# Matmul operands placed 32 and 96 bytes past the 2048-byte remainder of the weight tiles in SBUF

## What is computed

```python
x = x + mixed(mamba(h @ w_in), attention(h @ w_in)) @ w_mix_out
x = x + (silu(h @ w_ffn_gate) * (h @ w_ffn_up)) @ w_ffn_down
h = h + norm(diff_attention(norm(h)))
h = h + norm(conv_ffn(norm(h)))
h = h + norm(forgetting_attention(norm(h), k, v, c))
h = h + norm(conv_ffn(norm(h)))
```

## Time and profile before

| | us |
|---|---|
| median of 3 runs (lowest, highest) | 2476.02 (2474.82, 2476.4) |
| the profiled execution's own time | 2476.41 |
| its span in the trace | 2474.6 |
| TensorE matmul busy | 2439.0 (99%) |
| GpSimd busy | 1618.5 (65%) |
| VectorE busy | 1330.5 (54%) |
| ScalarE busy | 746.7 (30%) |

### The profile page before, as it was taken

How to read it: one execution, slowest core, us unless ns; L and a number is a source line. 1 busy time by engine, 2 the same in 40 slices (tenths; PEclk the granted TensorE clock), 3 DMA queues, 4 the chain that set the end, 5 groups by cost and what they waited for, 6 DMA issues and landing times.

```text
span 2474.6 us, 38549 instructions
## 1 busy us (share of the span) xinstructions
PE 2439.0 (99%) x13513; PEld 2002.5 (81%) x13520; DVE 1330.5 (54%) x1980; ACT 746.7 (30%) x1369; POOL 1618.5 (65%) x1548
## 2 busy tenths in 40 slices
PE   9999999999999999999999899999999999999999
PEld 7888888888778888888877688888877777888887
DVE  8777775535326333211555569785173344788822
ACT  3564552011232111101344433331042233333301
POOL 8756665755557777776544368887763434888874
PEclk9999999999999999999999999999999999999999
DMA  5433434333324333333322123333222222333331
GB/s 163 126 90 107 115 100 142 104 82 86 81 73 128 96 95 97 97 97 92 110 64 65 47 82 97 97 97 98 82 86 86 77 65 65 94 97 97 95 97 64
DMA packets 238100, 231.18 MB, mean 93 GB/s; under 512 B 16064, under 2 KB 230592, under 8 KB 237976
## 3 DMA queue, kind: packets, MB, share of 16 engines
q1 hardware_dynamic: 214528, 206.82, 28.7%
q10 hardware_dynamic: 23448, 22.61, 3.3%
HBM read 225.06 MB, written 4.84 MB: 93 GB/s over the span
## 4 chain that ended last, share of the span: by engine, by line
PE 71%; ACT 1%; DVE 1%; issue 0%; DMA 0%; SPq 0%; DVEq 0%; ACTq 0%
PE PS L682 42%; PE PS L673 5%; PE PS L674 5%; PE PS L677 5%; PE PS L666 4%; PE PS L757 3%; PE AUX L1008 2%; PE AUX L1052 1%; PE AUX L1064 1%; PE AUX L1069 1%; PE AUX L785 0%; PE AUX L791 0%; PE AUX L1029 0%; PE AUX L1011 0%; ACT opA_hi L1149 0%
## 5 line engine op out<-in xcount | busy, mean ns | idle before, releaser
L632 POOL TENSOR_TENSOR wlo<-raw,whi 128x512 fp32r<-128x512 f32 x772 | 1063.7, 1378 | 64.4
L630 POOL TENSOR_SCALAR whi<-raw 128x512 fp32r<-128x512 f32 x772 | 557.0, 721 | 766.9 <-issue 418.0
L682 PE MATMUL PS<-opA_hi,whi 128*128 128x512 f32 x1312 | 524.4, 400 | 0.9 <-DVE cu L1595 0.8
L682 PE MATMUL PS<-opA_hi,wlo 128*128 128x512 f32 x1312 | 511.7, 390 | 0.0
L682 PE MATMUL PS<-opA_lo,whi 128*128 128x512 f32 x1312 | 511.0, 390 | 0.0
L682 PEld LDWEIGHTS PS<-opA_hi,whi 128*128 128x128 f32 x1312 | 246.4, 188 | 59.9 <-issue 7.5
L682 PEld LDWEIGHTS PS<-opA_hi,wlo 128*128 128x128 f32 x1312 | 246.2, 188 | 53.0
L682 PEld LDWEIGHTS PS<-opA_lo,whi 128*128 128x128 f32 x1312 | 246.6, 188 | 49.6 <-issue 1.2
L2045 DVE SCALAR_TENSOR_TENSOR facc<-fu,vec,facc 128x512 f32<-128x512 f32 x176 | 216.8, 1289 | 15.8 <-ACT facc L1401 15.8
L673 PE MATMUL PS<-opA_hi,whi 128*128 128x512 f32 x560 | 221.2, 395 | 1.6 <-DVE XT L1900 0.8
L674 PE MATMUL PS<-opA_hi,wlo 128*128 128x512 f32 x560 | 218.6, 390 | 0.0
(11 more groups left out here) (329 smaller groups left out, 3760.4 us busy)
## 6 DMA issues: line engine op xcount, KB each, us to landing
raw<-in_w_in_dram SPq DMA_DIRECT2D x184, 256.0 KB, 2.8
raw<-in_ffn_w_in_dram SPq DMA_DIRECT2D x176, 256.0 KB, 2.8
raw<-in_ffn_w_out_dram SPq DMA_DIRECT2D x88, 256.0 KB, 2.6
raw<-in_a_w_qkv_dram SPq DMA_DIRECT2D x48, 256.0 KB, 2.7
raw<-in_w_ffn_gate_dram SPq DMA_DIRECT2D x44, 256.0 KB, 2.8
raw<-in_w_ffn_up_dram SPq DMA_DIRECT2D x44, 256.0 KB, 2.8
raw<-in_w_ffn_down_dram SPq DMA_DIRECT2D x44, 256.0 KB, 2.7
acs_row<-acs_dram ACTq DMA_DIRECT2D x16, 512.0 KB, 5.8
```

Of the source, the lines that this page charges most:

```text
L630: nc.gpsimd.tensor_scalar(whi[slot][:], raw[raw_slot][:], 1.0, 1.0, ALU.mult, ALU.mult).then_inc(w_high, 1)
L632: nc.gpsimd.tensor_tensor(wlo[slot][:], raw[raw_slot][:], whi[slot][:].bitcast(F32), ALU.subtract).then_inc(slab_split, 1)
L682: last = nc.tensor.matmul(psum_fm(key, panel, m), a, b[:, k, :], start=k + n == 0, stop=k == total - 1 and n == 2)
```

## The change

`opA_at`, the mark behind the weight tiles, stays where it is. `opA_hi` now begins 32 bytes past it, and everything placed in order behind it in the first region moves by 32 bytes with it. `A0` is rounded up to the remainder of `opA_at` plus 96 bytes. `A0` was 128 bytes behind the end of `ident_bf` and is now 192 bytes behind that end, which has itself moved by 32, so that the whole region moves by 96 bytes. `raw`, `whi`, `wlo` and `XT` stay.

| tile | bytes past the weights' remainder by 2048, before | after |
|---|---|---|
| `raw`, `whi`, `wlo` | 0 | 0 |
| `opA_hi`, `opA_lo` | 0 | 32 |
| `yT`, `o1`, `mix`, `hid`, `opB`, `q2`, `k2`, `sc`, `pT` | 0 | 96 |
| `ident` | 320 | 352 |
| `XT` | 1856 | 1856 |

No instruction, wait, transfer or size is added, removed or reordered.

```diff
         KB = 1024
         ROW = 4 * S
+        OPERAND_STEP, REGION_STEP = 32, 96
         BASE = -(-nc.sbuf_base // 64) * 64
...
         opA_at = r.at
+        r.at += OPERAND_STEP
         opA_hi = r.put("opA_hi", [P, DC, S], F32R)
...
         ident_bf = r.put("ident_bf", [P, P], BF16)
-        A0 = r.at + (opA_at - r.at) % ROW
+        A0 = r.at + (opA_at + REGION_STEP - r.at) % ROW
```

## The result

The changed kernel takes 2524.32 us (median of 4 runs, 2522.76 to 2526.18) against 2476.21 for the kernel before (median of 4). The ratio is 1.0185, with a 95% interval of 1.0173 to 1.0197: 48 us slower. The forecast was 19 us faster with a range that ended at 2507, so both the direction and the range were wrong.

What follows compares the result with a forecast made beforehand. TensorE was taken as the bound, through the distance between matmul starts. The profiled 2476.4 us less 19.1 for weight products, all else zero, gave 2457.3, named as 2457; range over all cases 2385 to 2507, likeliest case 2385 to 2471.

Steps and rivals of the forecast that it cites:

- What bounds the kernel: TensorE busy 2439.0 of 2474.6 us at full clock, longest wait sum 5.6 us; time can come only from matmul starts.
- the two reads act on each other by their addresses: Weight products: moving-row read and weight load may collide in SBUF, giving some 11 ns excess; an offset shifts their meeting.
- the value for the weight products: All 7440 products of 512 columns and 2112 of 256: 2 ns less each, 19.1 us less.
- the nearest row on the gaining side: Line 666, 256 columns: 118 ns a step just after other work in place of 120, 2 ns less.
- The upper bound: Worst end for weight products: 4.7 ns more for each of 7440, 256-column form 4.2 us less, together 30.8 us more.
- the pace after other work: Line 682, 512 columns: 231.4 ns just after other work in place of the settled 226.7.
- Groups left out: Smaller groups of weight products, under a tenth more, not counted beside the 7440 and 2112.
- Rival (c): Feature-major products settle at the pace after other work, 4.7 ns more each: 2507 us; 25%, with 4% beyond 2507.
- Rival (b): Weight products lose the whole excess over the bf16 run, 107 us less: 2369 us; 9% with partial forms.
- Rival (a): Nothing changes, 2476 us: the excess belongs to fp32r, the weight switch or a self-restoring phase; 30%.
- The terms taken as zero: Attention and scan on TensorE (`AUX`, possibly 5 us either way), VectorE, ScalarE and GpSimd durations, and transfers: no change.
- GpSimd's slack: From 1500 to 1600 us GpSimd needs 2319 ns a slab, TensorE 2720; even at 215.5 ns products, 267 ns remain.

Runs made afterwards that it cites:

- the map: Five kernels with `opA`, the region, `hid` and `mix` at various own distances from the weights, against the kernel before: 2548.8, 2517.4, 2534.7, 2495.9 and 2546.7 us.

## Why the prediction was wrong, step by step

- **What bounds the kernel** was right: all of the time came from distances between matmul starts, and TensorE's longest sum of waits is 5.9 us, where it was 5.6.
- **That the two reads act on each other by their addresses** was right as a mechanism, and it was given as the reason for the term. Moving everything by 32 bytes changed nothing; moving one against the other changed the products that read both.
- **The step that failed** is the value for the weight products: "I take the value of the nearest row on the gaining side, 2 ns less for each of 9552". The sign came from an argument, that an offset avoids the collision at the common start. Measured is 6.7 ns more for the 512-column form at 32 and at 96 bytes, and 1.7 ns less for the 256-column form, whose row the 2 ns came from. The value was near for the 2112 products that it was read from, and was then carried over to 7440 products of the other form, for which the row beside it showed the opposite sign (231.4 against 226.7). By the rows each form should have kept its own sign. That the 256-column form came near its 2 ns is partly luck: at other distances its gain is between 0.4 and 4.5 ns.
- **The upper bound** was too low as well: 4.7 ns a product, the pace after other work, was taken as the worst. It was 6.7 here and up to 12.8 (at 244 bytes) in the map. The pace of a disturbed stretch was no limit for a settled one.
- **Groups left out.** "Smaller groups of the same kind, under a tenth more, I leave out": with them it is 8160 feature-major products. Some 5 us of the 51 come from those 720.
- **Rival (c)** named the place, the products, the sign and the count by stretch (434; measured 430), and had 25%, of which 4% for a time beyond 2507. It had the price too low. With 6.7 ns in place of 4.7 and all 8160 products its sum gives 2476.4 + 54.7 - 3.6 = 2527.5; the profiled span says 2520.9 and some 2 us around it. The difference is mainly the `opA` products near other work, some 1550, which were slower before already and lost 4.6 ns each.
- **Rival (b)**, the excess of 11 ns gone, has nothing for it: the 512-column form is never less than 13.3 ns over its columns, and the 256-column form is 6.7 over them at best, in the faster stretches at 64 bytes. **Rival (a)** was right about one thing, that the settled distance of before is a state of its own: it is exactly 32 cycles over the columns in both forms.
- **The terms taken as zero** were right: `AUX` work -1.1 us, the other engines' busy times within 1% of before, the wait for the `vr` transfer 2.4 us in place of 2.2, GpSimd's slack larger.
- **The Trainium skill** ("SBUF — State Buffer", "Who interferes with whom") has TensorE's two read ports independent and TensorE never waiting. By that the 14 kernels of the experiments would have run alike; they lie between 2474 and 2549 us with nothing but addresses changed. The measurement decides.

What stays open: which access waits for which, why the repeat is 256 bytes, and what picks one of the two paces at 64 bytes. A kernel whose products have no weight load beside them was not tried, so that the load is the partner follows from the run with moved low weights, not from taking it away. Nor was it tried whether a bf16 product depends on the distance.

## What to carry to other kernels

In this kernel back-to-back fp32r matmuls with a weight load each run at a pace that depends on the distance of the moving row to the stationary piece by 256 bytes; it was worth up to 3% of the time. Where 512 columns move, give both the same remainder by 256; where 256 columns move, measure, since that was the dearest of nine distances there. And when any tile in front of an operand changes its size, check that the distance has not moved, before an unrelated edit is blamed or praised for it. A busy share of 99% says nothing on this; count the matmuls in a settled stretch.

## What was not expected of the hardware

- A shift of one float (4 bytes) from distance 0 costs 10.5 ns for each 128 x 512 product (226.7 to 237.2), more than 32 bytes do (233.3).
- The distance of 64 bytes has two settled paces in one kernel, 113 and 118 ns for the 256-column products and 228.9 and 233.3 ns for the 512-column ones.
- Many settled paces are whole multiples of 16 cycles of 2.4 GHz over the columns: 113.3 and 120.0 ns (16 and 32 over 256), 226.7 and 233.3 ns (32 and 48 over 512).
- The two forms want different distances: 0 is the cheapest for the feature-major form and the dearest of nine for the token-major one.
